# The end of the retention stage, put in another order: last variance, halves of the second row, and two rows for the roots

## The reference, cut to what matters

```python
def retention(q, k, v):
    ...
    mu = jnp.mean(o, axis=-1, keepdims=True)
    var = jnp.mean(jnp.square(o - mu), axis=-1, keepdims=True)
    return ((o - mu) * lax.rsqrt(var + GN_EPS)).reshape(B, S, H * d)

def even_layer(x, norm_g, w_in, b_f, gn_g, w_out):
    ...
    o_r = (retention(hd(q_r, RET_HEADS), hd(k_r, RET_HEADS), hd(v_r, RET_HEADS)) * gn_g).astype(x.dtype)
    y = jnp.concatenate([o_f, o_r], axis=-1) * jax.nn.silu(z)
    return x + y @ w_out
```

## Time and profile before

| | |
|---|---|
| time before, median of 3 runs | 1551.98 us (1548.54 to 1552.15) |
| the profiled execution, its own time | 1551.94 us |
| its span on the core | 1550.2 us |
| mean granted TensorE clock | 0.982 |
| PE busy | 1472.9 us (95%) |
| DVE busy | 973.6 us (63%) |
| ACT busy | 883.6 us (57%) |

### The profile page before, as it was taken

How to read it: one execution, slowest core, us unless ns; L and a number is a source line. 1 busy time by engine, 2 the same in 40 slices (tenths; PEclk the granted TensorE clock), 3 DMA queues, 4 the chain that set the end, 5 groups by cost and what they waited for, 6 DMA issues and landing times.

```text
span 1550.2 us, 24973 instructions
## 1 busy us (share of the span) xinstructions
PE 1472.9 (95%) x10140; PEld 947.6 (61%) x10140; DVE 973.6 (63%) x1945; ACT 883.6 (57%) x1251; POOL 66.8 (4%) x144
## 2 busy tenths in 40 slices
PE   6999998999998999999998999989799999899998
PEld 3444485665467548485787666446485755466677
DVE  6723547888478566565668224577756336699974
ACT  6553456777554565454553453557454556678863
POOL 0000000000100000000010000001000000000000
PEclk9999999999999999999999999999899999999999
DMA  6323322111422434433325366511023332200002
GB/s 185 108 84 107 99 92 82 55 55 55 163 83 82 140 99 123 132 104 107 109 87 77 93 92 88 110 55 32 27 83 109 114 109 82 82 1 2 2 1 96
DMA packets 127362, 132.07 MB, mean 85 GB/s; under 512 B 9776, under 2 KB 124208, under 8 KB 127120
## 3 DMA queue, kind: packets, MB, share of 16 engines
q1 hardware_dynamic: 125056, 121.69, 28.2%
q0 software_dynamic: 2192, 8.80, 1.6%
HBM read 128.38 MB, written 2.10 MB: 84 GB/s over the span
## 4 chain that ended last, share of the span: by engine, by line
PE 76%; DVE 12%; ACT 5%; issue 3%; DMA 3%; POOL 0%; DVEq 0%; ACTq 0%; SPq 0%
PE bank L713 13%; PE bank L715 12%; PE bank L714 12%; PE bank L756 6%; PE bank L758 6%; PE bank L757 6%; PE bank L950 3%; PE bank L932 3%; DVE wring L1878 3%; PE bank L923 3%; PE bank L919 1%; ACT whigh L1278 1%; DMA wring<-in_even_w_in 1%; PE bank L832 1%; PE bank L1087 1%
## 5 line engine op out<-in xcount | busy, mean ns | idle before, releaser
L713 PE MATMUL bank<-xT,whigh 128*128 128x512 f16 x960 | 366.8, 382 | 10.1 <-DVE xT L2056 5.1
L715 PE MATMUL bank<-xT,wring 128*128 128x512 f16 x960 | 366.6, 382 | 0.0
L714 PE MATMUL bank<-xT,whigh 128*128 128x512 f16 x960 | 366.5, 382 | 0.0
L1878 DVE SCALAR_TENSOR_TENSOR wring<-wring,wsc,whigh 128x2048 f16<-128x2048 f32 x105 | 245.1, 2334 | 163.6 <-ACT whigh L1278 162.9
L1278 ACT ACTIVATE whigh<-wring,wsc 128x2048 f16<-128x2048 f32 x105 | 208.8, 1988 | 144.5 <-DVE wsc L1781 127.4
L1295 ACT ACTIVATE whigh<-wring 128x2048 bf16<-128x2048 f32 x105 | 199.0, 1895 | 120.6 <-DMA wring<-in_even_w_in 37.6
L756 PE MATMUL bank<-whigh,slab 128*128 128x256 f16 x800 | 218.0, 273 | 3.3 <-DVE wring L1878 1.8
L758 PE MATMUL bank<-whigh,slab 128*128 128x256 f16 x800 | 218.1, 273 | 0.0
L757 PE MATMUL bank<-wring,slab 128*128 128x256 f16 x800 | 218.0, 273 | 0.0
L713 PEld LDWEIGHTS bank<-xT,whigh 128*128 128x128 f16 x960 | 94.6, 98 | 126.3 <-issue 9.4
L715 PEld LDWEIGHTS bank<-xT,wring 128*128 128x128 f16 x960 | 94.5, 98 | 115.1 <-issue 3.3
(11 more groups left out here) (325 smaller groups left out, 2345.1 us busy)
## 6 DMA issues: line engine op xcount, KB each, us to landing
wring<-in_w_in SPq DMA_DIRECT2D x28, 1024.0 KB, 5.1
wring<-in_w_up SPq DMA_DIRECT2D x16, 1024.0 KB, 5.4
wring<-in_w_down SPq DMA_DIRECT2D x16, 1024.0 KB, 5.4
wring<-in_even_w_in SPq DMA_DIRECT2D x14, 1024.0 KB, 9.5
wring<-in_odd_w_in SPq DMA_DIRECT2D x14, 1024.0 KB, 5.2
wring<-in_w_a SPq DMA_DIRECT2D x4, 1024.0 KB, 5.2
wring<-in_w_out SPq DMA_DIRECT2D x4, 1024.0 KB, 6.0
wring<-in_even_w_out SPq DMA_DIRECT2D x4, 1024.0 KB, 5.2
```

The lines of the kernel that those rows point to most:

```text
L713: pe.matmul(bank, wh[:, k, wcol:wcol + width], xh[:, k, :], start=k == 0, stop=False)
L714: pe.matmul(bank, wh[:, k, wcol:wcol + width], xl[:, k, :], start=False, stop=False)
L715: mm = pe.matmul(bank, wl[:, k, wcol:wcol + width], xh[:, k, :], start=False, stop=k == KC - 1)
L1878: dve.scalar_tensor_tensor(low_of(i)[:, :, 0:m], loaded(i)[:, :, 0:m], wsc[:, n:n + 1], high_of(i)[:, :, 0:m], ALU.mult, ALU.subtract).the ...
```

## The change

Four edits, all in the stretch above. On TensorE the last variance is issued directly behind the last sums, ahead of the projection's first slot. On ScalarE the high half of row 5 goes ahead of the third root. On VectorE the low half of row 5 goes ahead of the third pair's products, and the low half of row 6 goes behind the fourth pair's products. The roots alternate between `scr[3]` and `scr[5]`, so root m waits for the product of pair m - 2 and not of m - 1.

```diff
@@ TensorE, retention() and its call
-                return lambda: variances(3)
+                variances(3)
...
-            last_variances = retention()
+            retention()
...
-            tok_and_norm("oe", ..., nlate=2, between=last_variances)
+            tok_and_norm("oe", ..., nlate=2)
@@ ScalarE
             def pair_root(m):
                 act.wait_ge(s_("rt_var"), m + 1)
-                if m >= 1:
-                    act.wait_ge(s_("yr"), m)
-                act.activation(scr[:, 3, :], ps[7][:, :], ACT.Sqrt, bias=eps[:, 2:3]).then_inc(s_("rt_rs"), 1)
+                if m >= 2:
+                    act.wait_ge(s_("yr"), m - 1)
+                act.activation(scr[:, 3 + 2 * (m % 2), :], ps[7][:, :], ACT.Sqrt, bias=eps[:, 2:3]).then_inc(s_("rt_rs"), 1)
             for m in range(5):
                 if m < 4:
                     ret_copies(m)
+                if m == 4:
+                    out_high("oe", 5, slab[5][:, 5, :], "yr", 2)
                 if m >= 2:
                     pair_root(m - 2)
                 if m >= 1:
                     pair_square(m - 1)
-                if m >= 3:
-                    out_high("oe", m + 1, slab[5][:, m + 1, :], "yr", m - 2)
+                if m == 3:
+                    out_high("oe", 4, slab[5][:, 4, :], "yr", 1)
             pair_root(3)
@@ VectorE
-                dve.reciprocal(scr[:, 3, :], scr[:, 3, :]).then_inc(dve_chain, 1)
+                root = scr[:, 3 + 2 * (m % 2), :]
+                dve.reciprocal(root, root).then_inc(dve_chain, 1)
...
             out_low("oe", 4, slab[5][:, 4, :])
+            out_low("oe", 5, slab[5][:, 5, :])
             retention_out(2)
-            out_low("oe", 5, slab[5][:, 5, :])
+            retention_out(3)
             out_low("oe", 6, slab[5][:, 6, :])
-            retention_out(3)
             out_low("oe", 7, slab[5][:, 7, :])
```

More of the change, by code:

```diff
@@ L1158, in _ @@
             pe.wait_ge(s_("fox_y"), 4)
-            last_variances = retention()
+            retention()
             pe.wait_ge(s_("rt_ea"), 12)
             pe.wait_ge(*out_made("oe", 6))
-            tok_and_norm("oe", ohalves["oe"], SA, "rms_o", normed, SB, 1, "kc", SA, out_made("oe", 8), nlate=2, between=last_variances)
+            tok_and_norm("oe", ohalves["oe"], SA, "rms_o", normed, SB, 1, "kc", SA, out_made("oe", 8), nlate=2)
             feat("vc", 2, xhalves, SB)
@@ L2431, in retention_out @@
                 dve.wait_ge(s_("rt_rs"), m + 1)
-                dve.reciprocal(scr[:, 3, :], scr[:, 3, :]).then_inc(dve_chain, 1)
+                root = scr[:, 3 + 2 * (m % 2), :]
+                dve.reciprocal(root, root).then_inc(dve_chain, 1)
                 dve.wait_ge(dve_chain, own(dve_chain))
-                dve.tensor_tensor(slab[5][:, 4 + m, :], scr[:, 4, :], scr[:, 3, :], ALU.mult).then_inc(s_("yr"), 1)
+                dve.tensor_tensor(slab[5][:, 4 + m, :], scr[:, 4, :], root, ALU.mult).then_inc(s_("yr"), 1)
             attention(FOX)
```

## The result

The changed kernel took 1541.88 us in the median of its first 8 runs (1535.79 to 1546.51), against 1550.65 of the kernel before (8 runs, 1548.54 to 1552.17): a ratio of 0.9949, 95% interval 0.9934 to 0.9965, so 0.35 to 0.66% faster. Over all runs of this study the means are 1542.41 (38 runs) and 1549.46 us (99 runs), a difference of 7.05 +- 1.01 us. The forecast was 1546.5 us, in a range from 1543.0 to 1552.0. One slow run of 1578.8 us, in the first series of the kernel with 18 spare matmuls further down, is left out of all means.

What follows compares the result with a forecast made beforehand. VectorE's list, held up by the late fourth variance and root, was taken to set the second slot's start: 1551.94 - 7.07 for the earlier start + 1.6 for the clock's toll = 1546.5 us, range 1543.0 to 1552.0.

Steps and rivals of the forecast that it cites:

- What bounds the stretch: From 1100 to 1119 us VectorE's list was called the path; starting row 7's low half 7.07 us earlier moves the second slot equally.
- Each step of the sum on the way to the second slot: Instruction times rebuilt on ScalarE, TensorE and VectorE, with the second slot starting at 1112.18 in place of 1119.25 us.
- the gap ahead of the second slot: TensorE was to end its 24 matmuls at 1109.8 us and stand idle 2.4 us until the second slot; before, 0.90 us.
- The small wait of 0.3 us for the high half of row 5: VectorE's low half of row 5 was to wait some 0.3 us for ScalarE's high half, a new wait.
- The two rows of roots: Alternating the rows for the third and fourth root was said to be worth about 0.1 us by itself.
- the clock's toll: TensorE's 2.4 us gap was to bring 3.4 us at 1.2 GHz into the second slot, costing 1.6 us; chance 0.44.
- the toll is hidden: Rival: the slow stretch falls in the first slot, where TensorE has 3 or 4 us to spare; 1544.9 us, chance 0.27.
- the start value: The sum started from the profiled execution, 1551.94 us; the median of the runs shown, 1551.98, was taken as agreeing.
- TensorE as the bound: Rival: slow matmuls make TensorE bound the first slot, starting the second only 3 us earlier; 1549 us, chance 0.09.
- given back later: Rival: a later wait hangs on something that does not move, so the 7 us become idle time; 1552 us, chance 0.13.
- the 14 that it would take to turn the sign: Slower rival: a slow stretch on the path longer than 14 us outweighs the 7.07 won; 1557 us, chance 0.07.

Runs made afterwards that it cites:

- the kernel with 18 spare matmuls: Changed kernel plus 18 unread matmuls behind the first slot's last 24, for `oe` only; mean 1540.06 us, ratios to the kernel before 0.9951 and 0.9935 in two series.
- Both moves that take the root off the path: Kernel before with only the last variance moved: mean 1543.62 us, ratio 0.9966; changed kernel with that variance put back behind the first tile: mean 1541.87 us, ratio 0.9952.
- the one with row 5 late: Changed kernel with both halves of row 5 back in their old places on ScalarE and VectorE; mean 1543.01 us, ratio to the kernel before 0.9953.
- the one with 50: Changed kernel plus 50 spare matmuls in the gap ahead of the second slot; mean 1542.57 us, ratio to the kernel before 0.9957.

## Why the prediction was right in its path and wrong in its number

*What bounds the stretch: right.* VectorE's list was the path, and the late fourth variance was what held it. Both moves that take the root off the path, made one at a time, give 5.97 and 7.07 us; the forecast for the two together was 7.07, and 7.08 was measured. One reading was loose, though the sum does not hang on it. Between 1100.6 and 1107.2 the path of the kernel before was not VectorE's list, as I wrote, but led over TensorE's 18 slow matmuls, the variance, the root and ScalarE's high half, while VectorE waited.

*Each step of the sum on the way to the second slot: right to 0.3 us.* Counted from the third variance, the fourth was to start 5.46 us later (5.37 measured), the projection 6.6 (6.33), the reciprocals were to start 4.76 us apart (4.84), the gap ahead of the second slot was to be 2.4 us (2.22), the second slot to start 21.15 us behind (21.14). The small wait of 0.3 us for the high half of row 5 measured 0.2. The two rows of roots were said to be worth 0.1 us and are worth 0.05.

*The step that failed: the clock's toll.* The prediction put it: "I take 1.6, since the nearest row (2.47 us idle) did bring it." Its size was right, 1.67 us where it falls. Its frequency was not: it came in two of five traces of the changed kernel, and in one of four of the kernel before, to which I had given none. In the mean that is 0.4 x 1.67 - 0.25 x 1.67 = 0.25 us net, in place of 1.6. I had reasoned from one trace that a gap of 2.5 us brings a slow stretch; five traces with the same gap of 2.2 us show that the gap alone does not decide it. In two of them the slow stretch lay in the first slot, where TensorE has time to spare, as my rival "the toll is hidden" had it; in one there was none. The frequency itself is loose: the five of eight of all traces with this gap would put the changed kernel's toll at 1.0 us and the net at 0.6.

*The other part of the miss: the start value.* The sum began at 1551.94 us, the profiled execution, and I called it confirmed by the median of three runs. The mean of 99 runs is 1549.46, so the base was 2.5 us too high. The distance won is 7.0 us between the means of four and five traces. With these and the net toll: 1549.46 - 7.0 + 0.25 = 1542.7 us, against a mean of 1542.41 in 38 runs. The forecast's excess over that mean, 4.1 us, is 2.5 from the base, 1.35 from the toll, and 0.3 that stay open. The agreement is closer than the numbers allow one to ask for, as the difference of the two means is itself known to 1 us only.

*The range.* Its lower end took the case without the toll and 2 us for the scatter. Single runs of the kernel before and of the changed one have a standard deviation of 2.5 to 2.8 us here, and the base was itself one draw of them. A range for the outcome would have had to take both into account, down to 1540.

*The rivals.* "The toll is hidden" was the nearest (1544.9, given 0.27), and two of five traces of the changed kernel show what it described. TensorE as the bound did not come true in the changed kernel, but did in the one with row 5 late. Nothing was given back later that shows in the outer parts, and the slow stretch behind the second slot lasted 3.4 us, far from the 14 that it would take to turn the sign.

*What stays open.* The two kernels with spare matmuls lie 2.4 and 3.0 us below what distance and base give them (1549.46 - 7.0 = 1542.5 for the one with 18, 1545.5 for the one with 50). The missing stretch explains 0.4 of that, as the base holds it in one of four traces (0.25 x 1.67). Their traces show a shorter way from kc to the end (390.7, 390.2 and 391.5 us), but kernels without spare matmuls show such values too (388.0, 391.0). The two series of the kernel with 18 differ from each other by 3.1 us in the mean, more than the rest that is to be explained, so I don't call any cause shown. Whether the slow stretch on the path is a net price of 1.67 us for the whole kernel stays open as well.

## What to carry to other kernels

Where one late instruction holds a chain, moving it and moving what is ahead of it are often two cures of the same wait: price them one at a time before adding them up. Take the distance between two marks inside the trace as the measure of a local edit, and the runs' mean for the whole: here the distance of the changed kernel repeated to 0.01 us, and that of the kernel before to 0.84, while the runs of either spread over 11. But look at what such a mark to mark distance leaves out: the slow stretch, when it came on the path, lay behind the second mark. And ask of every start value how many runs stand behind it; one profiled execution and two more were 2.5 us off, which is a third of the effect.

## What the runs showed of the hardware that I had not expected

The same idle gap of TensorE, 2.21 or 2.22 us at the same place of the same program, was followed by a stretch at 1.2 GHz on the path in two traces and not in three. In two of these three a stretch of the same length, 3.4 us, had come earlier, behind an idle time of 1.94 us, and cost nothing there. So what a slow stretch costs hangs on where it falls, and in this program that differs from run to run. With 18 spare matmuls in the gap it did not come on the path in either of two traces, which is too few to show that they keep it away.

The section "HAM oscillation — how this bites in real kernels" of the Trainium skill (TensorE: Matmul & The Clock Gate) warns that matmuls behind a long wait start slow; the waits of its own case are longer than these gaps. The traces agree that a slow start can follow a gap, at a price of 1.67 us up to the next stage where it lies on the path, and show besides that a gap of this size brings it there only in some of the runs.
